# Five pairs of upward FFN tiles by seven products of half size, and the branch gates' activation sums dealt out in single steps

## The reference, cut to what matters

```python
# first block: three branches (A, B, C), each with a gate of its own, then merged by "branch gates" gm
h = rms_norm(x, norm_gain)
proj = h @ w_in                       # (..., ga, gb, gc, gm) = split(proj)
gates = sigmoid(gm.reshape(B, S, 3, D))
merged = gates[0]*((ya*silu(ga)) @ w_up_a) + gates[1]*(...) + gates[2]*(...)
# second block, feed-forward part
def conv_ffn(h, w_up, conv_w, w_down):          # w_up: 1024 x 5632, w_down: 2816 x 1024
    gu = causal_dwconv(h @ w_up, conv_w)        # three taps along time, per channel
    g, u = jnp.split(gu, 2, axis=-1)
    return (jax.nn.silu(g) * u) @ w_down
x = x + conv_ffn(rmsnorm(x, norm_ffn_gain), ffn_w_up, ffn_conv_w, ffn_w_down)
```

## Time and profile before

| | us |
|---|---|
| median of 3 runs (1226.7 to 1228.06) | 1227.82 |
| the profiled execution | 1227.92 |
| its span, first to last instruction | 1225.8 |
| PE busy in the span | 1209.8 |
| DVE, ACT, POOL busy | 711.2, 607.9, 705.5 |
| mean granted clock of PE | 0.997 |

### The profile page before, as it was taken

How to read it: one execution, slowest core, us unless ns; L and a number is a source line. 1 busy time by engine, 2 the same in 40 slices (tenths; PEclk the granted TensorE clock), 3 DMA queues, 4 the chain that set the end, 5 groups by cost and what they waited for, 6 DMA issues and landing times.

```text
span 1225.8 us, 18317 instructions
## 1 busy us (share of the span) xinstructions
PE 1209.8 (99%) x6667; PEld 991.0 (81%) x6667; DVE 711.2 (58%) x1235; ACT 607.9 (50%) x1176; POOL 705.5 (58%) x538
## 2 busy tenths in 40 slices
PE   9999999999998999999999999999999999999997
PEld 7987777787876899987897777878888888889886
DVE  5554427757657777745597555434454445966224
ACT  6365535676633344455645665544444444333544
POOL 8673233263368776856384557446555655886842
PEclk9999999999999999999999999999999999999999
DMA  6332222222222333354142123333333332334332
GB/s 240 106 88 85 60 64 58 60 70 73 59 70 77 95 104 95 105 188 112 52 118 61 46 73 88 103 86 96 92 89 104 96 89 82 103 92 120 107 86 69
DMA packets 62432, 112.22 MB, mean 92 GB/s; under 512 B 6856, under 2 KB 11464, under 8 KB 62344
## 3 DMA queue, kind: packets, MB, share of 16 engines
q1 hardware_dynamic: 62200, 111.06, 31.7%
q10 hardware_dynamic: 144, 0.00, 0.0%
HBM read 108.87 MB, written 2.16 MB: 91 GB/s over the span
## 4 chain that ended last, share of the span: by engine, by line
PE 91%; DVE 5%; ACT 1%; POOL 1%; issue 1%; DMA 0%; SPq 0%; DVEq 0%; POOLq 0%; ACTq 0%
PE pb L1093 22%; PE pb L1094 22%; PE pb L1096 21%; PE pb L1146 3%; PE pb L1148 3%; PE pb L1147 3%; PE pb L1302 2%; DVE t7s L2034 2%; PE pb L1278 2%; PE pb L1155 2%; PE pb L1245 1%; PE pb L1216 1%; PE pb L1218 1%; PE pb L1217 1%; PE pb L1199 1%; PE pb L1197 1%
## 5 line engine op out<-in xcount | busy, mean ns | idle before, releaser
L2650 POOL TENSOR_TENSOR wlo<-raw,whi 128x512 fp32r<-128x512 f32 (+2 forms) x384 | 522.1, 1379 | 331.0 <-ACT whi L1495 330.0
L1093 PE MATMUL pb<-HH,whi 128*128 128x512 f32 x856 | 345.6, 404 | 1.0 <-DVE th L1971 1.0
L1094 PE MATMUL pb<-HL,whi 128*128 128x512 f32 x856 | 338.5, 395 | 0.0
L1096 PE MATMUL pb<-HH,wlo 128*128 128x512 f32 x856 | 337.5, 394 | 0.0
L1495 ACT ACTIVATE whi<-raw 128x512 fp32r<-128x512 f32 (+2 forms) x384 | 226.0, 615 | 105.1 <-PE pb L1096 54.7
L1093 PEld LDWEIGHTS pb<-HH,whi 128*128 128x128 f32 x856 | 161.3, 188 | 43.6 <-issue 4.6
L1094 PEld LDWEIGHTS pb<-HL,whi 128*128 128x128 f32 x856 | 161.1, 188 | 38.0 <-issue 2.9
L1096 PEld LDWEIGHTS pb<-HH,wlo 128*128 128x128 f32 x856 | 160.9, 188 | 37.5
L1959 DVE TENSOR_TENSOR pb<-pb,rff 128x512 f32<-128x512 f32 x44 | 30.8, 700 | 124.0 <-PE pb L1096 117.6
L1604 ACT ACTIVATE P<-P,stat 128x256 f32<-128x256 f32 (+3 forms) x96 | 50.6, 528 | 78.5 <-DVE stat L2212 56.1
L2650 POOL TENSOR_TENSOR fl<-cv,fh 128x512 fp32r<-128x512 f32 x22 | 28.9, 1315 | 86.4 <-ACT fh L1880 86.4
(11 more groups left out here) (459 smaller groups left out, 2526.0 us busy)
## 6 DMA issues: line engine op xcount, KB each, us to landing
raw<-in_wall SPq DMA_DIRECT2D x368, 256.0 KB, 2.8
raw<-in_wall SPq DMA_DIRECT2D x8, 260.0 KB, 3.0
X<-in_xT SPq DMA_DIRECT2D x8, 256.0 KB, 5.1
X<-in_xT SPq DMA_DIRECT2D x2, 1024.0 KB, 7.4
outT<-PP SPq DMA_DIRECT2D x8, 256.0 KB, 2.4
raw<-in_wall SPq DMA_DIRECT2D x10, 192.0 KB, 2.4
raw<-in_wall SPq DMA_DIRECT2D x9, 128.0 KB, 2.5
cst<-in_cst SPq DMA_DIRECT2D x1, 832.0 KB, 7.3
```

Source lines behind the costliest of these rows:

```text
L1093: pe.do.matmul(b, hi, xh[k], start=start, stop=False, skip_group_check=tile[0] == "down")
L1094: pe.do.matmul(b, hi, xl[k], start=False, stop=False, skip_group_check=tile[0] == "down")
L1096: m = pe.do.matmul(b, lo, xh[k], start=False, stop=stop, skip_group_check=tile[0] == "down")
L2650: g.do.tensor_tensor(lo, x, hi.bitcast(F32), ALU.subtract).then_inc(*up(name, point))
```

## The change

Three things, in one diff.

1. `t_sums` for kp 0 to 2 of the branch gates is taken apart into six `t_piece` steps each (two sums of high and low part, four subtractions), dealt out one by one in slots 1 and 5 of the tiles: kp 0 from the first gateC tile, kp 1 from the first gm tile, kp 2 from gate B's tile 1; each group's `t_parts` follows in the next slot. What is left over is issued after gate B.
2. Pairs j = 6, 9, 11, 13, 15 of the upward FFN tiles go by seven products. Their activation sums (`t_sums(3, kp)`) are made in j = 0 to 2: ACT writes scaled activations to two spare banks and a buffer, DVE takes four differences, the split follows half a tile later. The three banks of a pair are ("ffn", 0, j), ("cd", j), ("ffn", 1, j).
3. The steps `taps(1, j-1)` and `product(j-1)` of the tile before such a pair are issued behind its fifth product (S3), and no longer behind `scaled(0, j)`.

```diff
+UPS = (6, 9, 11, 13, 15)
+NUP = NGATE + len(UPS)
 def slot(self, i):
     if i in (3, 7):
         self.step()
+    elif i in (1, 5) and self.extra:
+        self.add(*self.extra.pop(0))
 def pair(self, p):
     for x in FACTORS:
         self.split_to(self.unit_of[p, x] + LOOK)
         self.add("product7", p, x)
+        if x == "S3" and NGATE <= p < NUP:
+            self.add("taps", 1, UPS[p - NGATE] - 1)
+            self.add("product", UPS[p - NGATE] - 1)
...
+        def pieces(kp):
+            self.extra += [("t_piece", kp, i) for i in range(6)] + [("t_parts", 0, kp)]
+        pieces(0)
         for t in range(4):
             gate("gateC", "yC", t)
+        pieces(1)
...
         for t in range(4):
             gate("gateA", "yA", t)
-            if t in (1, 3):
-                add("t_sums", 0, t // 2)
-            if t == 2:
-                add("t_parts", 0, 0)
         for t in range(4):
             gate("gateB", "yB", t)
-            if t < 2:
-                add(("t_parts", "t_sums")[t], 0, 1 + t)
+            if t == 0:
+                pieces(2)
         while self.background:
             self.step()
-        add("t_parts", 0, 2)
+        while self.extra:
+            add(*self.extra.pop(0))
...
+        sums_of = {(j, half): 2 * j + half - 1 for j, half in ((0, 1), (1, 0), (1, 1), (2, 0))}
         for j in range(NPAIR):
+            if j in UPS:
+                for t in (("ffn", 0, j), ("cd", j), ("ffn", 1, j)):
+                    take(t)
+                self.pair(NGATE + UPS.index(j))
             for half in range(2):
-                take(("ffn", half, j))
-                self.proj(("ffn", half, j), "ffn_up", 2816 * half + P * j)
+                if j not in UPS:
+                    take(("ffn", half, j))
+                    self.proj(("ffn", half, j), "ffn_up", 2816 * half + P * j)
                 add("scaled", half, j)
-                if (half, j) != (0, 0):
-                    add("taps", 1 - half, j - 1 + half)
                 if half:
+                    add("taps", 0, j)
                     add("swish", j)
-                elif j:
+                elif j and j not in UPS:
+                    add("taps", 1, j - 1)
                     add("product", j - 1)
+                if (j, half) in sums_of:
+                    for i in range(2):
+                        take(("ts", sums_of[j, half], i))
+                    add("t_sums", 3, sums_of[j, half])
+                if (j, half - 1) in sums_of or (j - 1, half + 1) in sums_of:
+                    add("t_parts", 3, 2 * j + half - 2)
...
 # PE, product7
+                if kind(p) == "up":
+                    if x == "A12":
+                        pe.wait_ge(*at("u2", p))
+                    elif x in ("A11", "S1", "A22"):
+                        free(tile)
 # ACT, product7
+                if kind(p) == "up" and x == "S2":
+                    a.wait_ge(*at("product7", p, x))
+                    a.wait_ge(*at("u3", p - 1))
+                    a.do.activation(U7, ps("ffn", 0, UPS[p - NGATE])[:, 0:H], ACT.Copy).then_inc(*up("a_c7", ("v0", p)))
 # DVE
+            def product_up(p, x):
+                if x == "S2":
+                    v.wait_ge(*at("v0", p))
+                    v.wait_ge(*at("product7", p, "S2"))
+                    plus(U7, ab[:, right], U7, ("u2", p))
+                elif x == "S3":
+                    v.wait_ge(*at("product7", p, "S3"))
+                    v.wait_ge(*last("v_c7"))
+                    plus(W8, cd[:, left], U7)
+                    plus(ZU, cd[:, right], U7, ("u3", p))
+                    v.wait_ge(*last("v_c7"))
+                    plus(e[:, right], cd[:, right], W8, ("empty", ("cd", j)))
+                    plus(e[:, left], e[:, left], ZU)
+                elif x == "S4":
+                    v.wait_ge(*at("product7", p, "S4"))
+                    plus(ab[:, right], ab[:, right], W8)
```

More of the change, by code:

```diff
@@ L72, in quarters @@
         mat, (one, two) = "win", (gm_col(*x) for x in PAIRS[p])
+    elif p < NUP:
+        mat, one, two = "ffn_up", P * UPS[p - NGATE], 2816 + P * UPS[p - NGATE]
     else:
-        mat, one, two = "ffn_dn", 2 * P * (p - NGATE), 2 * P * (p - NGATE) + P
+        mat, one, two = "ffn_dn", 2 * P * (p - NUP), 2 * P * (p - NUP) + P
     return {"A11": (mat, one, 0), "A22": (mat, two, 4), "A21": (mat, two, 0), "A12": (mat, one, 4)}
@@ L656, in second @@
                 self.hold(DOWN_BANK["tile"][7], ("down", 7))
-            self.pair(NGATE + n)
+            self.pair(NUP + n)
             add("down_out", 2 * n)
@@ L940, in sums_at, with kind @@
             return S7 if p < NGATE else S8
+        def kind(p):
+            return "gate" if p < NGATE else "up" if p < NUP else "down"
         T_AT = {"S1": 0, "S3": 1, "A22": 2, "S2": 3}
@@ L1109, in product7 @@
                 later = []
-                if p < NGATE:
+                if kind(p) == "up":
+                    g, (xhs, xls), (ths, tls), j = 3, (hh, hl), (THU, TLU), UPS[p - NGATE]
+                    tile, half = {"A11": (("ffn", 0, j), 0), "S2": (("ffn", 0, j), 1), "S1": (("cd", j), 0), "S3": (("cd", j), 1),
+                                  "A12": (("ffn", 0, j), 0), "S4": (("ffn", 0, j), 1), "A22": (("ffn", 1, j), 0)}[x]
+                    b, starts = ps(*tile)[:, H * half:H * half + H], x in ("A11", "S1", "A22", "S4")
+                    if x == "A12":
+                        pe.wait_ge(*at("u2", p))
+                    elif x in ("A11", "S1", "A22"):
+                        free(tile)
+                elif p < NGATE:
                     g, (xhs, xls), (ths, tls) = 0, (hh, hl), (TH7, TL7)
@@ L1886, in h4 @@
             def h4(d):
[L1887 removed]
+                a.wait_ge(*at("product7", NUP + 3, "S3"))
                 a.wait_ge(*at("x_down", d))
@@ L1941, in half_out @@
                 a.do.activation(rs4[:, c], rs4[:, c], ACT.Exp, scale=-0.5).then_inc(*up("a_norm", ("rs4", half)))
-            follow({"begin": begin, "split": split, "t_parts": t_parts, "product7": product7, "first": first, "square": square,
+            follow({"begin": begin, "split": split, "t_sums": t_sums, "t_parts": t_parts, "product7": product7, "first": first, "square": square,
                     "lambda": lam_exp, "norm1": norm1, "x_norm": x_norm,
@@ L2027, in split, with t_piece @@
                     weights("S4", arrived["A12"], sums["S2"], ALU.subtract)
+            def t_piece(kp, i):
+                x11, x12, x21, x22 = (TS7[kp][:, H * n:H * n + H] for n in range(4))
+                v.wait_ge(*at("values", *[("C", 7, 3), ("A", 3, 3), ("B", 7, 3)][kp:kp + 1]))
+                if kp == 2:
+                    v.wait_ge(*at("yA", 3))
+                if i < 2:
+                    n = kp + 4 * i
+                    v.wait_ge(*at("x_lo", n))
+                    v.wait_ge(*at("x_hi", n))
+                    dst, one, two, op = TS7[kp][:, T * i:T * i + T], hh[n].bitcast(F32), hl[n].bitcast(F32), ALU.add
+                else:
+                    v.wait_ge(*last("v_t7"))
+                    dst, one, two = ((x11, x12, x11), (x12, x22, x12), (x22, x22, x11), (x21, x21, x22))[i - 2]
+                    op = ALU.subtract
+                v.do.tensor_tensor(dst, one, two, op).then_inc(*up("v_t7", *[("t_raw", 0, kp)] * (i == 5)))
             def t_sums(g, kp):
-                ts, (xhs, xls) = (TS7, TS8)[g][kp], ((hh, hl), (FH, FL))[g]
+                ts = {0: TS7, 1: TS8, 3: TSU}[g][kp]
                 x11, x12, x21, x22 = (ts[:, H * i:H * i + H] for i in range(4))
@@ L2034, in step @@
                     v.do.tensor_tensor(dst, one, two, op).then_inc(*up("v_t7", *points))
+                if g == 3:
+                    left, right = slice(0, H), slice(H, T)
+                    one, two = (ps("ts", kp, i) for i in range(2))
+                    v.wait_ge(*at("t_scaled", kp))
+                    step(x11, one[:, right], x11, ALU.subtract, ("empty", ("ts", kp, 0)))
+                    step(x12, two[:, right], x12, ALU.subtract)
+                    v.wait_ge(*last("v_t7"))
+                    step(x22, two[:, right], x11, ALU.subtract)
+                    v.wait_ge(*last("v_t7"))
+                    step(x21, two[:, left], x22, ALU.subtract, ("t_raw", g, kp), ("empty", ("ts", kp, 1)))
+                    return
+                xhs, xls = ((hh, hl), (FH, FL))[g]
                 if g:
@@ L2057, in product7 @@
             def product7(p, x):
-                if p >= NGATE:
-                    return product8(p, x)
+                if kind(p) != "gate":
+                    return product8(p, x) if kind(p) == "down" else product_up(p, x)
                 one, two = PAIRS[p]
@@ L2559, in scaled @@
                 b = ps("ffn", half, j)
-                v.wait_ge(*at("full", ("ffn", half, j)))
+                if j in UPS:
+                    v.wait_ge(*last("v_c7"))
+                else:
+                    v.wait_ge(*at("full", ("ffn", half, j)))
                 v.wait_ge(*at("rff"))
```

(5 more changed lines are left out.)

52 lines of the change are left out of this document (42 added, 10 removed).

## The result

The changed kernel takes 1229.38 us (median of 20 runs, 1228.18 to 1230.29), the kernel before 1227.59 us (20 runs beside them). The ratio is 1.0017, 95% interval 1.0011 to 1.0024: 1.8 us slower, under the 0.2% at which the prediction set its bound, where 1218.2 us had been forecast and 1224.0 us was the upper end of the range. The profiled execution took 1229.61 us, its span 1227.8.

A forecast was written before the change was run, and what follows sets the result against it. TensorE (PE), busy 1209.8 of 1225.8 us, was taken as the bound, leaving its idle places, low clock or column count. Sum: 1227.92 - 5.38 + 0.4 - 6.25 + 1.5 = 1218.2 us, range 1215.6 to 1224.0.

The forecast's parts named there:

- Gate holes: In the branch gates, PE's two idle holes and the low clock behind the second would go, gaining 5.38 us.
- rival B: Second gate hole stays because kp 2 pieces delay the last gate, or softmax loses as much: 1222.4 us, chance 0.15.
- Pieces in the softmax: Gate-sum pieces between softmax steps of the last A rounds and of B would cost 0.4 us, ends 0 and 3.
- Seven products: In the FFN, five upward pairs at 9.90 us instead of 11.15 would save 1.25 us each, 6.25 us.
- The signs it named: Wrong if A12 gaps exceed 2 us or clock falls, PE awaits weights' low parts, or gates' last low part holds PE.
- Late pairs: FFN pairs 11, 13, 15: DVE late with U2 makes PE wait before A12, costing 1.5 us, 0 to 3.4.
- FFN sums: Activation sums made in FFN tiles j = 0 to 2 would be hidden, cost 0, up to 2 us.
- The contention rule: Two-SBUF-input VectorE and SBUF-reading GpSimd instructions exclude each other; in late FFN pairs at least 2.2 us lost, sum 1218.9.

## Why the prediction was wrong

- **Gate holes, -5.38: right.** Both closed, the clock stays at 1.00; this also settles rival B's half about group 2.
- **Pieces in the softmax, +0.4 with ends 0 and 3: the step that failed.** It cost 7.7 us. The slack was read from one round of B, 2.4 us from the end of a normalisation to PE's transposes. But the second half of the transposes waits for a bank as well, which DVE empties by reading the next round's first scores, in that round at 304.99 to 305.27; that leaves about 1 us, an estimate from these rows. And the pieces were priced as two per tile spread evenly. "Two per tile" is an order of issue. Behind a wait (ACT's W) they run in one lump, and the place where group 1 starts has the mask cast, three POOL splits and the first round of B together. "POOL is much less busy there" was said of the stretch; at this spot, 270 to 280 us, POOL is busy 9.36 of 10 us. The clock was not priced in this term at all, and it was 2.3 of the 7.7. Moving group 1 gave back 5.6 us and moving group 0 as well 1.6 more.
- **Seven products, -6.25: right.** Undisturbed pairs last 9.74 to 9.81, a little better than 9.90.
- **The signs it named.** "PE waits for low parts of weights instead" and new waits on DVE in the softmax stood there as what would make it wrong; both came.
- **Late pairs, +1.5 (0 to 3.4): failed in mechanism, and in size.** They lost 10.58 + 11.23 + 11.22 - 3 x 9.78 = 3.7 us. The lag of DVE was longer than worked out, 2.2 us for 0 to 1.6 (the scaling comes 2.4 us after the start of pair 13, for 0.2 undisturbed), and it strikes at S1 through ACT's and POOL's order, not at A12 through U2. U2 ends 8.2 us after the pair's start, the late end of the working, but PE, held at S1, comes to A12 only then. The working counted the taps behind S3 in DVE's length and took the splits that ACT has behind the tile's product as covered; putting the taps and the product back gave 2.2 us.
- **FFN sums, 0 (up to 2): failed.** 2.4 us up to pair 6 (2.7 between the medians, with the shorter pair 15). The 1.1 us of overrun was weighed against the look-ahead of the splits as a sum over four tiles; the trace has ACT standing 4.05 us for DVE's product at 834.23 and POOL behind ACT, so the look-ahead was used up. That spreading the sets cures it is shown; which of the two queues fell behind first was not tried by itself.
- **The contention rule.** In the softmax a 128x1 step of DVE takes 1.21 us at 284.55 while POOL splits from 283.21 on, and 0.15 us at 282.88 with POOL idle. The Trainium skill (SBUF — State Buffer, "Who interferes with whom") says that a VectorE instruction with two SBUF inputs contends with a GpSimd one that reads SBUF, and calls what they share an exclusive lock; the trace agrees, since the step ends 0.02 us after the splits. The prediction let POOL lengthen the pieces, but weighed the rule itself for the FFN only, and not for the small steps of the normalisations behind the pieces.

With the measured terms: 1227.9 - 5.4 + 7.7 - 5 x 1.37 + 3.7 + 2.4 = 1229.5, against 1229.4. Of the rivals, B named softmax rounds that lose as much as the second hole had, 4.2 us; nothing allowed for more. How the 7.7 divides between the pieces' own length, POOL's splits and the cast is known only as far as the cast's move shows (2.1 us of it) and for the hole that it left.

## What to carry to other kernels

Work dealt out in small steps goes where the engine's queue lets it go: behind a wait it arrives as a lump, so price it at the worst queue in the stretch, with the other engines of that spot (0.42 us of a piece cost 1.4 more by letting POOL's splits go first), and add the clock behind a hole as long as those of 2.5 us and more were here. A step put "in the gap" ahead of a sum that frees a bank is on that sum's path, and on the path of the in-order engine that takes its result. Room between the cheaper pairs was worth more here than another pair: five saved 5.5 us, six 5.1.

## What the runs showed of the hardware

Here PE's clock fell to the lower of its two levels at the holes of 2.56, 2.87 and 4.07 us (0.80 to 0.83 in the window), as at that of 2.49 us in the kernel before, and not at those of 1.65, 0.95 and 0.61; the lower clock cost 2.3 us more after the longest. A 1.29 us operation of POOL, moved beside two steps of DVE, lengthened them by 1.13 us.
